# Macaron encoder trunk: the merge recomputed with tokens on the partitions, gates and retention output as seven-product groups

## The reference

```python
for l in range(DEPTH):
    x = x + 0.5 * swiglu(rmsnorm(x, norm_ffn1[l]), ...)
    h = rmsnorm(x, norm_mix[l]); z = h @ w_in[l]
    rq, rk, rv, rg, dq, dk, dv, g_ret, g_dil = jnp.split(z, IN_SPLITS, axis=-1)
    y_ret = retention(rq, rk, rv, rg, ...) @ w_ret_o[l]          # 1024 -> 1024
    y_dil = dilated_attention(dq, dk, dv, ...) @ w_dil_o[l]      # 512 -> 1024
    gates = jax.nn.sigmoid(concat([g_ret, g_dil]) + b_gate[l])
    merged = gates[..., :D_MODEL] * y_ret + gates[..., D_MODEL:] * y_dil
    x = x + merged @ w_out[l]
    x = x + 0.5 * swiglu(rmsnorm(x, norm_ffn2[l]), ...)
```

## Time and profile before

| | |
|---|---|
| runs | 2584.44, 2584.5, 2586.0 us; median 2584.5 |
| the profiled execution | 2585.45 us, its span 2583.6 us |
| TensorE busy | 2573.9 us, 100% of the span |
| VectorE, ScalarE, GpSimd busy | 1901.9, 1163.3, 78.2 us |
| merge of layer 0 | from 741.27 to 949.37 us |
| granted clock of TensorE | 1.00 |

### The profile page before, as it was taken

One profiled execution on the slowest core, in us unless ns is written; L12 is line 12 of the kernel. 1 busy time (PEld: TensorE's weight loads), 2 busy tenths in 40 slices (PEclk: granted clock), 3 DMA queues, 4 the chain that ended last, 5 costly groups with the idle time before them and its releaser, 6 DMA issues.

```text
span 2583.6 us, 38836 instructions
## 1 busy us (share of the span) xinstructions
PE 2573.9 (100%) x14769; PEld 2280.4 (88%) x14769; DVE 1901.9 (74%) x2374; ACT 1163.3 (45%) x1787; POOL 78.2 (3%) x79
## 2 busy tenths in 40 slices
PE   9999999999999999999999999999999999999999
PEld 7999987888888888999989999878888888889998
DVE  8877868777775469777788778787776844697776
ACT  5433446556563234433443334565655622443332
POOL 1111001000000000000000000010000000000000
PEclk9999999999999999999999999999999999999999
DMA  5443243333343333333223332432422433333331
GB/s 185 149 123 116 66 156 89 103 113 89 104 151 113 96 111 122 99 105 98 98 82 123 97 97 74 147 96 89 128 89 89 156 118 97 114 115 98 100 107 54
DMA packets 231230, 281.50 MB, mean 109 GB/s; under 512 B 14644, under 2 KB 185057, under 8 KB 230829
## 3 DMA queue, kind: packets, MB, share of 16 engines
q1 hardware_dynamic: 225960, 270.63, 33.1%
q0 software_dynamic: 4512, 5.04, 0.7%
q10 hardware_dynamic: 646, 4.31, 0.4%
HBM read 265.52 MB, written 19.04 MB: 110 GB/s over the span
## 4 chain that ended last, share of the span: by engine, by line
PE 96%; DVE 2%; issue 0%; ACT 0%; DMA 0%; SPq 0%; DVEq 0%
PE proj L663 24%; PE proj L665 24%; PE proj L664 24%; PE acc L663 6%; PE acc L665 6%; PE acc L664 6%; PE acc L1017 1%; DVE ring_lo L1899 1%; PE acc L944 1%; PE acc L965 0%; PE acc L927 0%; ACT ring_hi L1313 0%; PE acc L928 0%; DMA raw<-in_w_in 0%; DVE h_lo L2385 0%
## 5 line engine op out<-in xcount | busy, mean ns | idle before, releaser
L663 PE MATMUL proj<-h_hi,ring_hi 128*128 128x256 f32 (+1 forms) x1632 | 548.4, 336 | 2.2 <-DVE h_lo L1907 1.5
L665 PE MATMUL proj<-h_hi,ring_lo 128*128 128x256 f32 (+1 forms) x1632 | 544.0, 333 | 0.0
L664 PE MATMUL proj<-h_lo,ring_hi 128*128 128x256 f32 (+1 forms) x1632 | 543.7, 333 | 0.0
L663 PE MATMUL proj<-y_hi,ring_hi 128*128 128x256 f32 (+1 forms) x1504 | 463.5, 308 | 0.0
L665 PE MATMUL proj<-y_hi,ring_lo 128*128 128x256 f32 (+1 forms) x1504 | 463.0, 308 | 0.0
L664 PE MATMUL proj<-y_lo,ring_hi 128*128 128x256 f32 (+1 forms) x1504 | 462.9, 308 | 0.0
L1351 ACT ACTIVATE ring_hi<-raw 128x1024 fp32r<-128x1024 f32 (+1 forms) x175 | 209.9, 1203 | 359.9 <-PE acc L665 194.6
L663 PEld LDWEIGHTS proj<-h_hi,ring_hi 128*128 128x128 f32 x1632 | 310.1, 190 | 35.2 <-DVE h_lo L1907 1.9
L665 PEld LDWEIGHTS proj<-h_hi,ring_lo 128*128 128x128 f32 x1632 | 309.9, 190 | 30.5
L664 PEld LDWEIGHTS proj<-h_lo,ring_hi 128*128 128x128 f32 x1632 | 310.2, 190 | 28.7
L665 PEld LDWEIGHTS proj<-y_hi,ring_lo 128*128 128x128 f32 x1504 | 287.2, 191 | 13.8
(11 more groups left out here) (299 smaller groups left out, 4197.6 us busy)
## 6 DMA issues: line engine op xcount, KB each, us to landing
raw<-in_ffn_gate SPq DMA_DIRECT2D x88, 512.0 KB, 3.6
raw<-in_ffn_up SPq DMA_DIRECT2D x88, 512.0 KB, 4.2
raw<-in_w_in SPq DMA_DIRECT2D x136, 256.0 KB, 3.7
raw<-in_w_in SPq DMA_DIRECT2D x60, 512.0 KB, 5.1
raw<-in_ffn_down SPq DMA_DIRECT2D x56, 512.0 KB, 4.3
work<-in_ffn_down SPq DMA_DIRECT2D x32, 512.0 KB, 5.9
raw<-in_w_out SPq DMA_DIRECT2D x16, 512.0 KB, 4.3
raw<-in_w_ret_o SPq DMA_DIRECT2D x12, 512.0 KB, 4.2
```

Of the source, the lines that this page charges most:

```text
L663: pe.matmul(o, s_hi, m_hi, start=start, stop=False, skip_group_check=onto)
L664: pe.matmul(o, s_hi, m_lo, start=False, stop=False, skip_group_check=onto)
L665: return pe.matmul(o, s_lo, m_hi, start=False, stop=stop, skip_group_check=onto)
```

## The change

The merge is rewritten on all five engines. Results have tokens on the partitions; three groups of seven products follow each other: both gates from h (first the dilated one, GD, then the retention's, GR), then the retention's output product from y (RET), each in the order M1, M2, M5, M3, M6, M7, M4, with a 2048-word piece of weights per product.

- Bias: it can't be ScalarE's bias per partition any more. For both gate groups M1 and M5 get two one-row matmuls more per block: a stationary column of ones, and the bias row (split in hi and lo, the second half as a difference) moving. SyncE loads the rows, GpSimd makes difference, rounding and rest (`gate_bias`).
- Weight sums: T1 of the first group is made by GpSimd, all others by VectorE.
- The inputs y: block sums S1, S3, N2, S4 by GpSimd from the spilled heads' y, reloaded to `work` and `raw`; split by ScalarE and VectorE (`y_op`). The fourth head's y is no longer spilled.
- Dilated output: two units of four products (4 depth pieces), gated and summed block by block (`dil_part`).
- The sums are turned by TensorE (`turned`, 8 x 4 transposes of 128 x 128) into acc banks, split from there (`merged_hi`, `merged_lo`), and W_out goes through 8 depth pieces for outputs 0 to 3, then for 4 to 7 (`out_part`); each output is added to x once, not four times.
- Counters that were per head are now per group (3 more in each layer), which changes wait values in `heads` and nothing else there.

The core of the diff (TensorE's list, and the others' order):

```diff
-MERGE_TILES = [2, 1, 1, 1, 1, 2, 2, 2, 8, 2, 2] + [2, 8, 2, 2, 2] * (KT // 2 - 2) + [8]
+MERGE_TILES = [2] * (3 * PROD) + [4] * 7
+MERGE_ORDER = (M1, M2, M5, M3, M6, M7, M4)
...
+            def token_product(u, kind, b, hi, lo, rows=None):
+                op, bank, adds = HEAD_PRODUCTS[kind]
+                out, t = PB[bank + b][:, :], slice(b * P, (b + 1) * P)
+                for k in range(4):
+                    c = slice(k * SEQ, (k + 1) * SEQ)
+                    last = three(out, hi[op][:, k, t], lo[op][:, k, t], w_hi[u.slot][:, c], w_lo[u.slot][:, c], ...)
+                if rows is not None:
+                    one = ones_r[0:1, 0:1].to_broadcast([1, P])
+                    pe.matmul(out, one, y_hi[0:1, rows, :], start=False, stop=False)
+                    last = pe.matmul(out, one, y_lo[0:1, rows, :], start=False, stop=True)
...
+                def group(g, hi, lo, inserts):
+                    for j, kind in enumerate(MERGE_ORDER):
+                        u = at(PROD * g + j)
+                        begin(u)
+                        for b in (0, 1):
+                            if kind == M1:
+                                pe.wait_ge(head_c21, 2 * G + b + 1)
+                            elif kind == M2:
+                                pe.wait_ge(head_c12, 2 * G + b - 1)
+                            elif kind == M5:
+                                pe.wait_ge(head_c11, 2 * G + b + 1 + BANK_CREDIT)
...
+                            else:
+                                pe.wait_ge(head_c22, 2 * G + b + 1)
+                            if g != RET_GROUP and kind in (M1, M5):
+                                pe.wait_ge(row_step, 6 * l + 3 * g + 3)
+                            token_product(u, kind, b, hi, lo, rows)
...
+                group(GD_GROUP, op_hi, op_lo, {(1, 0): [kq 0, 1], (1, 1): [kq 2, 3], (2, 0): [kq 4, 5],
+                                               (2, 1): [scores 0, 1], (3, 0): [scores 2], (3, 1): [scores 3], (5, 0): [dil_move]})
+                group(GR_GROUP, op_hi, op_lo, {(0, 0): [turn 0, 1], (0, 1): [turn 2, 3], (1, 0): [values, near]})
+                group(RET_GROUP, ret_hi, ret_lo, {})
+                dil_part(0)
+                dil_part(1)
+                out_part(0, 0, 0, 4)
+                out_part(1, 0, 4, 8)
+                out_part(2, 4, 0, 4)
+                out_part(3, 4, 4, 6)
+                out_part(4, 4, 6, 8)
```

GpSimd, after its four heads:

```diff
+                pool.wait_ge(ret_s, 4 * H + 4)
+                gate_bias(GD_GROUP)
+                pool.wait_ge(rqk_landed, ...)
+                pool.wait_ge(block_landed[B12], ...)
+                pool.tensor_tensor(raw[:, 1, :], raw[:, 1, :], raw[:, 0, :], ALU.subtract).then_inc(t_made, 1)
+                pool.wait_ge(ret_sum, H + 1)
+                gate_bias(GR_GROUP)
...
+                pool.tensor_tensor(y_src[S1], y21, y_src[A22], ALU.add).then_inc(y_summed, 1)
+                pool.tensor_tensor(y_src[S3], y21, y_src[A11], ALU.subtract).then_inc(y_summed, 1)
+                pool.tensor_tensor(y_src[N2], y_src[A11], y_src[S1], ALU.subtract).then_inc(y_summed, 1)
+                pool.tensor_tensor(y_src[S4], y_src[A12], y_src[N2], ALU.add).then_inc(y_summed, 1)
```

VectorE's order in the merge, where `lo(k)` is the rest of piece k (0 is M1 of GD, taken in the head), `t1` to `t4` the weight sums, `c11`, `c12`, `c22` the bank sums:

```diff
+                g = GD_GROUP
+                qk_factors(H); lo(1); k_scale x 4; lo(2); c11(g, 0); c11(g, 1); lo(3); t2(g); ret_gate(H)
+                dil_softmax(H, 0); lo(4); dil_softmax(H, 1); t3(g); dil_softmax(H, 2); lo(5); dil_softmax(H, 3); t4(g)
+                dil_spread(H, l); lo(6); dil_gather(H); c22(g, 0); dil_combine(H); c22(g, 1); lo(7); dil_scale x 4
+                g = GR_GROUP
+                t1(g); lo(8); c12(GD, 0); c12(GD, 1); lo(9); c11(g, 0); c11(g, 1); lo(10); t2(g); dil_out_lo(l); y_op(A12)
+                lo(11); t3(g); y_op(S1); lo(12); y_op(A11); t4(g); c12(g, 0); lo(13); c22(g, 0); c22(g, 1); y_op(N2)
+                c12(g, 1); lo(14); y_op(S4); y_op(S3)
+                g = RET_GROUP
+                t1(g); lo(15); y_op(A22); lo(16); c11(g, 0); c11(g, 1); y_op(DIL_OP); lo(17); t2(g); gated(M2, 0)
+                lo(18); t3(g); gated(M2, 1); lo(19); t4(g); c12(g, 0); c12(g, 1); lo(20); c22(g, 0); c22(g, 1); lo(21)
+                gated(M3), gated(M7), gated(M4), two blocks each
...
```

More of the change, by code:

```diff
@@ L104, in unit @@
 def unit(layer, fixed, loop=0, loop_units=0, loop_tiles=0):
-    def turns(last):
-        return sum(1 for i in range(MERGE_BASE + 1, last) if i % 2 == fixed % 2)
     return Unit(layer * ITEMS_LAYER + FFN_ITEMS + loop * loop_units + fixed, fixed % 2,
-                layer * turns(MIX_UNITS) + turns(fixed),
                 layer * TILES_LAYER + FFN_TILES + loop * loop_tiles + sum(MIX_TILES[:fixed]), MIX_TILES[fixed - 1] if fixed else 8)
@@ L1165, in heads @@
                     squares_sum(H)
-                pe.wait_ge(head_c22, 2 * H + 2)
+                pe.wait_ge(head_c22, 2 * (H + 3 * l) + 2)
                 head_product(u, M4, 1)
             def merge(l):
-                def gate(u, bank, t=0, width=2 * P, between={}):
-                    tile_cols(u, bank, t, width=width, between=between)
-                def product(u, bank, k0, k1, col, between={}, fresh=None):
-                    for k in range(k0, k1):
-                        for step in between.get(k, ()):
-                            step()
-                        if fresh is not None:
-                            pe.wait_ge(y_lo_ready, 5 * l + fresh(k))
-                        c = (k - col) * P
-                        last = three(bank[:, :], w_hi[u.slot][:, c:c + P], w_lo[u.slot][:, c:c + P],
-                                     y_hi[:, k, :], y_lo[:, k, :], k == k0, k == k1 - 1)
-                    last.then_inc(tiles_done, 1)
@@ L1228, in merge @@
-                M0, H = KT * l, 4 * l + 3
-                kq = lambda i: lambda: qk_turn(H, i)
-                turn = lambda b: lambda: dil_turn(H, b)
-                values = lambda b: lambda: dil_values(H, b)
-                scores = lambda b: lambda: dil_scores(H, b)
-                near_values = lambda: dil_near(H)
-                at = lambda k: unit(l, MERGE_BASE + k)
-                u = at(0)
-                begin(u)
-                pe.wait_ge(head_c21, 2 * H + 1 + BANK_CREDIT)
-                gate(u, PB[0], 0, between={7: [kq(0), kq(1)]})
@@ L1802, in merge @@
                 dil_exps(H, 3)
+                u2(g, 1)
+                hi(6)
                 dil_factors(H)
-                gate(M0 + 1, 1, PB[3])
-                split(at(5))
+                hi(7)
+                for kind in (M2, M7):
+                    for b in (0, 1):
+                        gate(g, kind, b)
+                act.wait_ge(ret_y, 4 * H + 4)
+                gate(g, M4, 0)
+                gate(g, M4, 1)
+                g = GR_GROUP
+                hi(8)
                 for i in range(NB):
@@ new lines, in merge @@
+                m1(g, 1)
+                hi(9)
+                dil_out_hi(H, l)
+                gate(GD_GROUP, M3, 0)
+                gate(GD_GROUP, M3, 1)
+                hi(10)
+                m5(g, 0)
+                m5(g, 1)
+                y_op(A12)
+                hi(11)
+                y_op(S1)
+                y_op(A11)
+                hi(12)
+                u2(g, 0)
+                u2(g, 1)
+                hi(13)
+                y_op(N2)
+                for b in (0, 1):
+                    gate(g, M2, b)
@@ new lines, in merge @@
+                hi(14)
+                y_op(S4)
+                for kind in (M3, M7):
+                    for b in (0, 1):
+                        gate(g, kind, b)
+                y_op(S3)
+                gate(g, M4, 0)
+                gate(g, M4, 1)
+                g = RET_GROUP
+                hi(15)
+                y_op(A22)
+                m1(g, 0)
+                m1(g, 1)
+                hi(16)
+                y_op(DIL_OP)
+                hi(17)
+                act.wait_ge(y_lo_ready, Y_OPS * l + Y_ORDER.index(A22) + 1)
@@ L1838, in merge @@
+                m5(g, 0)
+                m5(g, 1)
+                hi(18)
+                hi(19)
+                u2(g, 0)
+                u2(g, 1)
+                hi(20)
+                hi(21)
+                hi(22)
+                hi(23)
+                for f in range(4):
+                    merged_hi(f)
+                hi(24)
+                for f in range(4, 8):
+                    merged_hi(f)
+                hi(25)
+                hi(26)
+                hi(27)
                 first_split(l, 1)
-                merged_hi(M0 + KT - 1, 1)
```

890 lines of the change are left out of this document (517 added, 373 removed).

## The result

| | before | changed |
|---|---|---|
| median of the runs | 2584.9 us (2584.4 to 2586.0) | 2638.5 us (2636.9 to 2639.4) |
| ratio, 95% interval | | 1.0206 (1.0193 to 1.0219) |
| span of the profiled execution | 2583.6 us | 2637.1 us |
| TensorE busy / chain that ended last | 100% / TensorE 96% | 98% / TensorE 88% |

Slower by 53.7 us, 26.8 per layer. The forecast was 2612 with a range up to 2627: the side was right, the size was half of what came. In experiments 5, 8 and 13 one of the six executions took two to five times the time of the others; it is in their medians, which would be 0.2 us lower without it.

A forecast was written before the change was run, and what follows sets the result against it. TensorE, busy 2573.9 of 2583.6 us, was taken as the bound. Per layer -9.1 work, +14.3 waits, +5.6 and +3.2 GpSimd holds make +14.0, +28.0 for two layers: 2612 us, range 2574 to 2627.

The forecast's parts named there:

- TensorE's work: Merge: 72 fewer wide matmuls save 16.3 us; one-row matmuls add 3.6 and turns 3.6; net 9.1 us less per layer.
- hold: GpSimd's sums make VectorE wait whole instructions: 5.6 us in the first group, 3.2 in the second, per layer.
- the move: First gate group: the maxima's move, behind VectorE's fourth sum, makes TensorE wait 1.5 us.
- the split chain: M6, M7, M4: sum, rounding and rest take 6.4 us against 5.44 per product; all waits together 14.3 us per layer.
- My 3.2 us for the y sums: Second group: GpSimd's first three y sums could hold VectorE 2.45 us each, 7.3 in all; 3.2 taken, bounds 0 and 8.
- rival 4: Granted clock stays at 1.2 GHz after long gaps, with every hold at its upper bound: 2628 to 2634 us; chance 0.08.
- my main case: Whole kernel: less TensorE work, but waits and GpSimd's holds give +14.0 us per layer, 2612 us; chance 0.40.
- costed at nothing: Work of ScalarE, SyncE, the merged sums' way and the FFN's start taken to lie beside other work, at 0 us.
- 1 (no hold): Merge: the waits come but GpSimd does not hold VectorE; +5.2 us per layer, 2595 us; chance 0.20.
- 2 and 3 (waits under 11 us): Merge waits per layer: about 3 us, giving 2572 us, chance 0.20; or 8 to 11, giving 2582 to 2588, chance 0.12.
- 5: Matmuls don't fall by 72, so the 9.1 us saving becomes less; inside the range, no chance of its own.
- The sign I named for being wrong on the chain: TensorE's idle time in the changed profile, expected at 40 to 50 us, would be under 18 us.

The follow-up runs named there:

- experiment 5: Changed kernel with ScalarE's scaling of x rows 0 to 3 earlier and VectorE's remainders of them ahead of the FFN's first split: 2632.5 us.
- experiment 8: Changed kernel with the edits of experiment 2, experiment 3 and experiment 5 plus 9, 9 and 10 filler matmuls in three remaining gaps: 2603.4 us, ratio 1.0072.
- Experiment 13: Changed kernel with VectorE's first half of the C22 sum ahead of each group's 7th-product split, and T4 earlier in the second group: 2628.8 us.
- experiment 2: Changed kernel with GpSimd's T1 weight sum cut to 8 of 2048 columns, the rest left out: 2628.9 us.
- experiment 1: Changed kernel with 60 filler matmuls per layer on TensorE ahead of the merge's four long waits: 2628.3 us.
- experiment 3: Changed kernel with GpSimd's four y sums in the second group cut to 8 columns, the rest left out: 2625.0 us.
- experiment 7: Changed kernel without the 16 one-row bias matmuls per layer, GpSimd still making the rows: 2631.9 us.
- experiment 4: Changed kernel with only ScalarE's scaling and squaring of x rows 0 to 3 moved ahead of its last copies: 2638.0 us.
- experiment 14: Changed kernel with the edits of experiment 5, experiment 6, experiment 12 and Experiment 13 together, nothing left out, no fillers: 2610.5 us, ratio 1.0099.
- experiment 6: Changed kernel with the first group's T1 made on VectorE behind M2's split, not on GpSimd: 2626.9 us.
- experiment 12: Changed kernel with the four y sums on VectorE, spread over places where it had idled, not on GpSimd: 2632.7 us.

## Why the prediction was right and wrong

**Right: TensorE's work, but for one term.** 72 wide matmuls fewer and 3.2 us of turns came as said. The one-row matmuls were taken at 0.23 us "like any other", from rows of matmuls over all 128 partitions; they follow one another at 0.33, so 5.3 in place of 3.6. It fell between the bounds given (0 and 0.4).

**Right: which waits, where and how long.** Forecast and trace, chain and hold taken together: M2 of the first group 7.4 and 6.7, the move 1.5 and 1.2, M4 2.5 and 2.2, M6 of the second group 3.6 and 3.9, M7 1.0 and 0.7, M4 2.7 and 2.6, the third group 3.3 and 2.5. In all 23.1 against 19.7 us. Laying the durations of single instructions out in the order of the lists was worth its trouble. Experiment 2 takes 4.4 us of M2's wait away with T1 and leaves 2.3; I had 5.6 and 1.8. The near match of the 2.3 is in part luck: up to 1.9 of it is the split of 736.48, held by GpSimd's row instruction; I had priced those instructions only as what makes M1 late (up to 1.4 us), and M1 waited 0.32 for its split. One reading of these waits was wrong: I took them as what the split chain must cost (6.4 against 5.44). Experiment 13 took 3.8 us of them away by order and gave 1.8 back at other places.

**Right: GpSimd holds VectorE for whole instructions.** One exception to how I put it: "only instructions of VectorE with both inputs in SBUF are held". The first square-root step has one input, an int32 tensor in SBUF, and took 4.83 us beside T1. The Trainium skill (SBUF — State Buffer, "SBUF: two separate sides") says that the port pair is locked exclusively and for the whole instruction, and it names VectorE's instructions in a 2-port perf mode beside those with two SBUF inputs. The ends of the rows agree with the lock, 745.15 for T1 and 745.44 for the step; whether the step ran in such a mode no run shows. My 3.2 us for the y sums, "somewhat under half" of the 7.3 that single holds give, was too low: leaving them out was worth 6.8, of which 3.9 idle.

**Wrong, and the step that failed: rival 4.** I wrote that "after a gap as long as the 5 to 8 us before M2 the granted clock may stay at 1.2 GHz", priced it at 1.5 for each 3 us, tied it to every hold at its upper bound, and gave it 0.08. It needed neither. The clock fell behind waits of 6.7, 3.9, 2.6 and 2.2 us, four times in a merge, for 7.0 us of slow matmuls per layer, of which 5.1 came back with experiment 1. The waits that call it up were in my own sum. A term of my main case had been made a rival. With it the sum would have read 2622 (by the 5.1) to 2626 (by the 7.0), still under 2627; the two terms that follow, costed at nothing, carry it past that.

**Wrong: costed at nothing.** "The FFN starts on x rows 0 to 3, which end a whole unit sooner": true, and the rest of them was made behind a split that waits for the FFN's first block, with row 4's sum behind both. 2.4 us per layer by the starts, 3 by experiment 5. I looked at when the rows end and not at what stands ahead of their next step in VectorE's order.

**Wrong: a wait costs its idle time.** 50 matmuls of the merge start behind a wait or another kind of work, 12 before: 4.2 us per layer that I gave no row, beyond 0.4 for the turns. This is read from the trace; no experiment tried it alone.

Against the forecast of +14.0 per layer these make +7.0 (clock), +3.8 (restarts), +2.4 (FFN's start), +1.7 (one-row), +1.0 (the head's end, the turns of q and k), -3.4 (waits): 26.5, where the starts give 27.3 and the medians 26.8. **The other rivals.** 1 (no hold) falls with experiments 2 and 3; 2 and 3 (waits under 11 us) fall with the account; 5 falls with the count of matmuls. The sign I named for being wrong on the chain, under 18 us of idle time in all, did not come: the two merges have 39. What stays open: what the 1.9 us by which the bias rows' instruction lengthens the split at 736.48 cost in time (no run left it out), and the 4 us by which the single gains exceed their joint one.

## What to carry to other kernels

When a change opens waits on a TensorE that had none, price each with its idle time, 0.2 to 0.3 us of restart, and the slow stretch behind it; look for the last in the granted clock, because it is booked as busy. Price a saving by what stands behind it: ahead of a wait much of it goes into the wait (3.7 of 5.3 us in experiment 7). And when a step moves to an engine with a fixed order, ask what is queued behind it there: the same four sums on VectorE cost 1.9 us or were worth 5.8 by place alone.

## What the runs showed of the hardware

- The granted clock was at the 1.2 GHz level behind idle times of 2.1 to 8.3 us, for 2.7 to 6.1 us (6 to 14 matmuls). No wait of 1.9 us or less had a slow stretch behind it in the merges read. Between 2.1 and 3.2 us it goes either way: 2.23 us in front of the same matmuls had one in the changed kernel and none in experiment 4, experiment 14 had none behind 2.30, 2.12 and 2.48 us in its first merge and one behind 2.31 and 2.13 in its second, and experiment 1 had none behind 3.17 and one behind 3.16. Every wait of 3.86 us or more had one. Runs of one kernel differ with it: in experiment 6 the mean granted clock was 0.997 in the run of 2623.4 us and 0.994 in that of 2629.7. In experiment 12 it was 0.996 at 2624.8 us and 0.995 at the others, too little to account for all of the 8 us.
- GpSimd's sums take 1.3 us for 512 words per partition and 2.4 for 1024. T1, of 2048, shows 5.49 us, but ends 4.5 us after the VectorE split that it overlaps. For 8 words experiment 3 has 0.20 us with no VectorE instruction beside it (the row below), and experiment 2 has 1.29 us where the sum ends at 741.04 with VectorE's split (740.97): there it was GpSimd that was held.

```profile
838.35 0.20 POOL L724 TENSOR_TENSOR work<-work,raw 128x8 f32<-128x8 f32 x1 [9.28 <-DVE y_lo L2715]
```

- One row is not cheaper than 128 on GpSimd either: its sum of 1 x 1024 in the bias rows takes 2.40 us. A one-row matmul (contraction over one partition, 512 columns) takes 0.33 us from start to start in place of 0.227.
